# Two conditioned mixers with later parameter loads, new hand-written orders, and output splits on GpSimd

## What is computed

```
first_block, for each of 2 layers:
  x = layer_norm(ALPHA * x + 0.5 * swiglu_ffn(x, ffn1_w_gu[l], ffn1_w_down[l]), ...)
  x = layer_norm(ALPHA * x + hybrid_mixer(x, w_in[l], w_out[l], attn_sinks[l], ...), ...)
  x = layer_norm(ALPHA * x + 0.5 * swiglu_ffn(x, ffn2_w_gu[l], ffn2_w_down[l]), ...)
second_block, for each of 2 layers:
  mod = silu(c) @ w_ada[l] + b_ada[l];  shift, scale, gate = split(mod, 3)
  h = x * (1 + scale) + shift
  parts = split(h @ w_in[l], SPLIT_POINTS)
  o_a = mla_attention(...)        # latent attention, 6 heads
  o_b = dilated_attention(...)    # 6 heads
  o_c = sparse_attention(...)     # 4 heads, keys chosen by an indexer's top 64
  y = concatenate([o_a, o_b, o_c]) * silu(p_gate)
  x = layer_norm_2(ALPHA * x + (1 + gate) * (y @ w_out[l]), ln_g[l], ln_b[l])
```

## Time and profile before

| | us |
|---|---|
| median of 3 runs | 1343.25 (1341.85 to 1345.84) |
| the profiled execution, its own time | 1349.49 |
| its span, first to last instruction | 1347.7 |
| PE busy | 1321.4 (98%) |
| DVE busy | 1016.7 (75%) |
| ACT busy | 678.1 (50%) |
| POOL busy | 105.6 (8%) |
| DMA from HBM | 263.13 MB |

### The profile page before, as it was taken

One profiled execution on the slowest core, in us unless ns is written; L12 is line 12 of the kernel. 1 busy time (PEld: TensorE's weight loads), 2 busy tenths in 40 slices (PEclk: granted clock), 3 DMA queues, 4 the chain that ended last, 5 costly groups with the idle time before them and its releaser, 6 DMA issues.

```text
span 1347.7 us, 18984 instructions
## 1 busy us (share of the span) xinstructions
PE 1321.4 (98%) x7172; PEld 1119.2 (83%) x7172; DVE 1016.7 (75%) x1597; ACT 678.1 (50%) x1069; POOL 105.6 (8%) x153
## 2 busy tenths in 40 slices
PE   8999999999999999999999999999999999999997
PEld 7888888787888878888887888888888988798985
DVE  6676678886777777776778886687685689967887
ACT  6444445634544445344447445444355577456581
POOL 1011000011011100111010110111100000100000
PEclk9999999999999999999999999999998999999999
DMA  7976756437777557777564457777576443484530
GB/s 266 320 234 219 243 182 202 125 117 250 235 235 234 188 180 266 235 234 222 167 222 154 125 181 242 265 234 234 178 245 209 149 126 126 141 239 149 152 121 32
DMA packets 199402, 265.46 MB, mean 197 GB/s; under 512 B 21584, under 2 KB 144592, under 8 KB 198800
## 3 DMA queue, kind: packets, MB, share of 16 engines
q1 hardware_dynamic: 187600, 223.65, 51.8%
q0 software_dynamic: 11712, 40.60, 8.7%
HBM read 263.13 MB, written 1.07 MB: 196 GB/s over the span
## 4 chain that ended last, share of the span: by engine, by line
PE 84%; DVE 9%; DMA 4%; ACT 1%; issue 1%; SPq 0%; DVEq 0%; ACTq 0%
PE ps L791 26%; PE ps L793 25%; PE ps L792 25%; PE ps L860 4%; DVE w_lo L1266 3%; DMA w_raw<-in_w_in 2%; DMA w_raw<-in_ffn_w_gu 2%; PE ps L1004 1%; DVE arena L1557 1%; PE ps L1065 1%; PE ps L1039 1%; DVE small L1555 1%; DVE few_first L1295 1%; DVE y L1294 1%; ACT w_hi L1094 1%
## 5 line engine op out<-in xcount | busy, mean ns | idle before, releaser
L1266 DVE TENSOR_TENSOR w_lo<-w_raw,w_hi 128x1024 fp32r<-128x1024 f32 (+3 forms) x424 | 499.9, 1206 | 152.0 <-ACT w_hi L1094 148.9
L1094 ACT ACTIVATE w_hi<-w_raw 128x1024 fp32r<-128x1024 f32 (+3 forms) x424 | 432.5, 1046 | 244.5 <-DMA w_raw<-in_ffn_w_gu 126.2
L791 PE MATMUL ps<-w_hi,col_hi 128*128 128x512 f32 (+2 forms) x1024 | 396.3, 387 | 5.0 <-DVE w_lo L1273 2.6
L793 PE MATMUL ps<-w_hi,col_lo 128*128 128x512 f32 (+2 forms) x1024 | 391.3, 382 | 0.0
L792 PE MATMUL ps<-w_lo,col_hi 128*128 128x512 f32 (+2 forms) x1024 | 391.1, 382 | 0.0
L791 PEld LDWEIGHTS ps<-w_hi,col_hi 128*128 128x128 f32 x1024 | 192.7, 188 | 43.6 <-DVE w_lo L1266 4.6
L793 PEld LDWEIGHTS ps<-w_hi,col_lo 128*128 128x128 f32 x1024 | 192.4, 188 | 37.3
L792 PEld LDWEIGHTS ps<-w_lo,col_hi 128*128 128x128 f32 x1024 | 192.8, 188 | 34.0
L791 PE MATMUL ps<-w_hi,lat_hi 128*128 128x512 f32 (+2 forms) x544 | 209.0, 384 | 0.0
L793 PE MATMUL ps<-w_hi,lat_lo 128*128 128x512 f32 (+2 forms) x544 | 206.6, 380 | 0.0
L792 PE MATMUL ps<-w_lo,lat_hi 128*128 128x512 f32 (+2 forms) x544 | 206.3, 379 | 0.0
(11 more groups left out here) (148 smaller groups left out, 1182.9 us busy)
## 6 DMA issues: line engine op xcount, KB each, us to landing
w_raw<-in_ffn_w_gu SPq DMA_DIRECT2D x352, 256.0 KB, 4.4
w_raw<-in_w_in SPq DMA_DIRECT2D x108, 512.0 KB, 4.6
w_raw<-in_ffn_w_down SPq DMA_DIRECT2D x88, 512.0 KB, 4.9
mod<-in_w_ada POOLq DMA_DIRECT2D x32, 768.0 KB, 7.4
w_raw<-in_w_out SPq DMA_DIRECT2D x24, 512.0 KB, 4.6
norm_g<-in_ln_g POOLq DMA_DIRECT2D x8, 512.0 KB, 4.4
norm_b<-in_ln_b POOLq DMA_DIRECT2D x8, 512.0 KB, 6.0
w_raw<-in_w_out SPq DMA_DIRECT2D x16, 256.0 KB, 4.4
```

What stands on the lines that cost most here:

```text
L791: pe.matmul(dst, a_hi, b_hi, start=start, stop=False)
L793: return pe.matmul(dst, a_lo, b_hi, start=False, stop=stop)
L1094: act.activation(half_of(w_hi[j], n, h), half_of(raw[j], n, h), ACT.Copy).then_inc(hi_ready, 1)
L1266: tt(half_of(w_lo[j], n, h), half_of(raw[j], n, h), half_of(w_hi[j], n, h).bitcast(F32), ALU.subtract)\
```

## The change

It has five parts.

1. **Orders.** `MIX1_ORDER` and `MIX2_ORDER` are replaced. Mix1 keeps all its jobs. On PE its only exchanges are `trret:Q:0` with `score:W:2`, `trret:Q:1` with the three VR rows, and `row:GR:0:0` with `turn:W:2`. In mix2, PE's list changes in four places: `T:QI:0` goes ahead of `turn:B:0` and the VBX rows ahead of `score:B:0`; `mix:B:2` goes up, `trA:2` to `trA:5` come in a row, and `T:QC:1` comes between `score:A:1` and `turn:A:0` with `score:A:0` ahead of `T:QC:0`; `T:G:2` goes from ahead of `mix:A:2` and `turn:C:0` to behind them; at the end, both `xt` jobs of the next stage go ahead of `out:2:1` and `out:3:1`. The splits of ACT and DVE move with them, and high and low parts need no longer stand in the order of the units.
2. **GpSimd.** In mix2 the low parts of the four output units, eight halves, are subtracted by POOL (jobs `po:out/q:h`) with a semaphore of their own, and PE waits on that one for them. They stand in POOL's list ahead of and behind `modload`.
3. **params.** In mix2 the loads of gain and bias wait for `ropeA:0` instead of the translated x. In POOL's list `gateload` and `modload` stand behind them.
4. **table2.** It is loaded with the params of stage 5, an ffn stage, instead of at the start of stage 6. Stage 6's shift and scale therefore get a place in the arena instead of the table.
5. **Narrow pieces.** A piece of at most 64 columns is loaded whole with half 0. VBX has four transfers a unit instead of six, KI two instead of four, with the same bytes.

```diff
-hi:VBX/0:0 hi:VBX/0:1 row:L0:1:1 lo:QB/1:1 lo:QB/2:0 row:L1:1:0 row:L1:1:1 lo:QB/2:1 T:QB:0 xlate:0 hi:VBX/1:0
-lo:VBX/0:0 lo:VBX/0:1 sq:1 T:QB:1 lo:VBX/1:0 xlate:1 params hi:VBX/1:1 hi:QI/0:0 hi:QI/0:1 T:QB:2 latent:1
-trlat:0:0 trlat:0:1 hi:QI/1:0 hi:QI/1:1 score:B:0 lo:VBX/1:1 lo:QI/0:0 hi:KI/0:0 weigh:B:0 lo:QI/0:1 hi:KI/0:1
-row:VBX:0:0 trlat:1:0 trlat:1:1 row:VBX:0:1 row:VBX:1:0 row:VBX:1:1 lo:QI/1:0 lo:QI/1:1 turn:B:0 score:B:1 idxw:0
...
+hi:VBX/1:1 T:QB:0 T:QB:1 xlate:0 hi:QI/0:0 lo:VBX/1:0 latent:0 hi:QI/0:1 lo:VBX/1:1 lo:QI/0:0 xlate:1 lo:QI/0:1
+sq:1 T:QB:2 latent:1 params hi:QI/1:0 trlat:0:0 row:VBX:0:0 row:VBX:0:1 trlat:0:1 trlat:1:0 hi:QI/1:1 hi:KI/0:0
+row:VBX:1:0 score:B:0 lo:QI/1:0 trlat:1:1 hi:KI/0:1 row:VBX:1:1 hi:UQ/0:0 T:QI:0 hi:UQ/0:1 weigh:B:0 turn:B:0
...
+topk:0:0 topk:0:1 gateload topk:0:2 lo:QC/1:1 hi:G/0:0 trA:5 hi:G/0:1 hi:G/1:0 hi:G/1:1 topk:0:3 row:VC:1:0
+score:A:0 topk:1:0 T:QC:0 lo:G/0:0 topk:1:1 hi:G/2:0 weigh:A:0 score:A:1 lo:G/0:1 hi:G/2:1 topk:1:2 hi:G/3:0
+hi:G/3:1 T:QC:1 hi:out/0:0 turn:A:0 weigh:A:1 score:A:2 lo:G/1:0 lo:G/1:1 lo:G/2:0 hi:out/0:1 lo:G/2:1 T:G:0
+mix:A:0 lo:G/3:0 hi:out/1:0 turn:A:1 score:C:0 lo:G/3:1 weigh:A:2 weigh:C:0 T:G:1 mix:A:1 turn:A:2 topk:1:3
+score:C:1 po:out/0:0 mix:A:2 gate:1:0 weigh:C:1 gate:0:0 po:out/0:1 po:out/1:0 hi:out/1:1 turn:C:0 ycols:0:0
+T:G:2 T:G:3 gate:0:1 mix:C:0 gate:1:1 turn:C:1 +modload +fold gate:0:2 hi:out/2:0 ycols:1:0 ycols:1:1 mix:C:1
+ycols:0:1 ycols:0:2 po:out/1:1 po:out/2:0 po:out/2:1 po:out/3:0 hi:out/2:1 hi:out/3:0 out:0:0 gate:1:2 hi:out/3:1
+po:out/3:1 +lo:L0/0:0 out:1:0 out:2:0 +hi:L0/0:0 +hi:L0/0:1 out:3:0 ycols:1:2 norm:0 out:0:1 out:1:1 +hi:L0/1:0
...
                 for h in range(2):
-                    for q, (tensor, l, r0, c0, w, at_) in enumerate(pieces):
+                    for q in pieces_of((s, name), h):
+                        tensor, l, r0, c0, w, at_ = pieces[q]
...
+                        if w <= NARROW:
+                            tiles = slice(0, ks)
...
-                if kind == "params":
-                    if s > 0:
+                if kind == "po":
+                    n, h = NUMBER[job[1:3]], job[3]
+                    pool.wait_ge(hi_ready, at["high_part", job[1:]])
+                    pool.tensor_tensor(half_of(w_lo[SLOT[n]], n, h), half_of(raw[SLOT[n]], n, h),
+                                       half_of(w_hi[SLOT[n]], n, h).bitcast(F32), ALU.subtract).then_inc(po_ready, 1)
+                elif kind == "params":
+                    if KIND[s] == "mix2":
+                        pool.wait_ge(rope_a_done, at["ropeA", ("ropeA", s, 0)])
+                    elif s > 0:
                         pool.wait_ge(x_ready, at["x_ready", (s, 1, 1)])
...
+                    if s == FIRST2 - 1:
+                        pool.dma_start(table[:, 0:T2], t["table2"]).then_inc(tables_in, 16)
```

More of the change, by code:

```diff
@@ L208 @@
 MIX1_ORDER = """
[L209 to L218, removed]
@@ new lines @@
+score:W:1 hi:VR/0:1 weigh:W:0 row:KR:0:0 row:KR:0:1 row:KR:1:0 lo:VR/0:0 hi:VR/1:0 weigh:W:1 hi:VR/1:1 turn:W:0
+lo:VR/0:1 row:KR:1:1 lo:VR/1:0 hi:GR/0:0 hi:GR/0:1 mix:W:0 turn:W:1 lo:VR/1:1 rot:Q:0 hi:GR/1:0 hi:GR/1:1 params
+rot:Q:1 hi:out/0:0 row:VR:0:0 trret:Q:0 rot:K:0 lo:GR/0:0 attn:0 score:W:2 weigh:W:2 lo:GR/0:1 row:VR:0:1
+row:VR:1:0 row:VR:1:1 rot:K:1 trret:Q:1 trret:K:0 mix:W:1 hi:out/0:1 ret:0 row:GR:0:0 lo:GR/1:0 hi:out/1:0
+turn:W:2 lo:GR/1:1 lo:out/0:0 ret:1 mix:W:2 attn:1 retmix:0 gn:0 lo:out/0:1 trret:K:1 row:GR:0:1 ret:2 gnx:0
@@ L231 @@
[L231 to L245, removed]
+hi:L1/1:0 lo:L1/1:0 lo:L1/1:1 row:L0:0:0 row:L0:0:1 row:L1:0:0 hi:L1/1:1 xt:1:0 lo:QB/0:0 hi:QB/0:0 xt:1:1
@@ new lines @@
+lo:QI/1:1 lo:KI/0:0 lo:KI/0:1 score:B:1 lo:UQ/0:0 T:QI:1 weigh:B:1 hi:UQ/1:0 T:KI:0 hi:UQ/1:1 lo:UQ/0:1
+hi:UKV/0:0 score:B:2 weigh:B:2 mix:B:0 idxw:0 idxw:1 idx:0 turn:B:1 hi:UKV/0:1 hi:VC/0:0 lo:UQ/1:0 lo:UQ/1:1
+hi:VC/0:1 lo:UKV/0:0 row:UQ0:0:0 row:UQ0:1:0 hi:QC/0:0 mix:B:1 lo:UKV/0:1 hi:QC/0:1 idx:1 turn:B:2 lo:VC/0:0
+row:UQ1:0:0 row:UQ1:1:0 hi:QC/1:0 hi:QC/1:1 row:UV:0:0 lo:VC/0:1 lo:QC/0:0 row:UV:1:0 ropeA:0 ropeA:1 idx:2
+row:UK:0:0 ropeK:0 mix:B:2 ropeK:1 lo:QC/0:1 row:UK:1:0 trA:0 trA:1 row:VC:0:0 lo:QC/1:0 trA:2 trA:3 trA:4
@@ L339, in with_splits @@
         assert at <= first[u]
-        places[at] += [(kind, *u, h) for h in range(2) for kind in ("hi", "lo") if (kind, *u, h) not in placed]
+        places[at] += [(kind, *u, h) for h in range(2) for kind in ("hi", "lo")
+                       if (kind, *u, h) not in placed and (kind, ("po", *u, h)) not in {("lo", q) for q in placed}]
     return [q for p, job in zip(places, jobs) for q in p + [job]]
@@ L346, with pieces_of @@
 NUMBER = {u: n for n, u in enumerate(UNITS)}
-for kind_ in ("hi", "lo"):
-    assert [q[1:] for q in JOBS if q[0] == kind_] == [(*u, h) for u in UNITS[FIRST_UNITS:] for h in range(2)], "split in order"
+HALVES = [(*u, h) for u in UNITS[FIRST_UNITS:] for h in range(2)]
+for kinds_ in (("hi",), ("lo", "po")):
+    assert sorted(HALVES.index(q[1:]) for q in JOBS if q[0] in kinds_) == list(range(len(HALVES))), "each half is split once"
 SLOT = [n % SLOTS for n in range(len(UNITS))]
 AFTER = [n - SLOTS if n >= SLOTS else None for n in range(len(UNITS))]
+NARROW = 64
+def pieces_of(u, h):
+    return [q for q, piece in enumerate(unit_shape(*u)[2]) if h == 0 or piece[4] > NARROW]
 LANDINGS = []
@@ L353 @@
     before = [LANDINGS[m] for m in range(n_) if SLOT[m] == SLOT[n_]]
-    LANDINGS.append((before[-1] if before else 0) + (16 * len(unit_shape(*u_)[2]) if n_ >= FIRST_UNITS else 0))
+    LANDINGS.append([(before[-1][h_] if before else 0) + (16 * len(pieces_of(u_, h_)) if n_ >= FIRST_UNITS else 0)
+                     for h_ in range(2)])
 def gu_bank(s, r, i):
@@ L403, in count_jobs @@
             held, step, readers, stage, buffers = {}, None, {}, s, []
+        if kind in ("hi", "lo", "po"):
+            COUNT.add("low_part" if kind == "lo" else "pool_part" if kind == "po" else "high_part", job[1:])
         got = unit_of(job)
```

38 lines of the change are left out of this document (23 added, 15 removed).

## The result

The changed kernel took 1365.68 us in the median of 4 runs (1365.13 to 1366.23), the kernel before beside it 1344.55 us (4 runs, 1341.85 to 1349.59). The ratio is 1.0159, with a 95% interval of 1.0134 to 1.0183. The forecast was 1337.4 us with a range up to 1344.5: wrong in direction, and by 28.3 us. The profiled execution took 1365.8 us, its span is 1364.0 us, so it stands for the median, unlike the one of before, which lay 6.2 us above its own.

What follows compares the result with a forecast made beforehand. PE was taken as the bound, busy 1321.4 of 1347.7 us, leaving at most 26.3 us to win. Terms of -7.2, -2.8, -1.1, +2.8, +0.8 and +1.6 sum to -5.9 us: 1343.25 to 1337.4 us, range 1331.5 to 1344.5.

Steps and rivals of the forecast that it cites:

- R2: Rival, mix2 stages: POOL's subtractions and DVE's two-operand SBUF reads hold each other up; 1341.8 us, chance 0.18.
- B: At `turn:A:0`, both mix2 stages: two low parts fewer on DVE ahead of `weigh:A:0` remove a wait; -2.8 us.
- C: End of stage 6: eight low parts leave DVE, so the wait behind the next stage's norm goes; -1.1 us.
- A: At `turn:B:0`, both mix2 stages: later parameter loads and new order remove PE's wait and the lower clock; -7.2 us.
- D: New waits at `mix:A:2` and `turn:C:0` in both mix2 stages, as `T:G:2` no longer covers them; +2.8 us.
- E: Four `trA` in a row, mix2 stages: the third and fourth wait for ACT's copy of the bank; +0.8 us.
- F: Output products, mix2 stages: POOL's subtractions, taken at 2.4 us each, come 0.8 us late per stage; +1.6 us.
- R3: Rival: POOL's subtraction takes 4 us or more, PE waits at out/2:1 to out/3:1; 1350.2 us, chance 0.07.
- Mix1 and the loads: Mix1 stages and the parameter, table and narrow loads at their new places: no new PE waits, costed at 0.
- R4: Rival at `turn:B:0`: narrow pieces, not POOL's loads, delay QI/1, and KI lands late; 1341.4 us, chance 0.08.

Runs made afterwards that it cites:

- the memsets: Kernel without POOL's subtractions, plus 24 POOL fills in stage 7 that write SBUF, read nothing and serve nobody: 1339.53 us, one run.

## Why the prediction was wrong

**The step that failed is the price of R2.** The sum credits B and C with DVE's full relief and puts nothing for DVE being held up by POOL; that stands only in the rival R2, at 4.5 us. The mechanism was named there, with the two-operand instructions of DVE, and the mark by which to know it ("longer than their 1.22 us"). The SBUF — State Buffer page of the Trainium skill (Who interferes with whom) states an exclusive lock between a DVE instruction with two SBUF inputs and a GpSimd instruction that reads SBUF, not one that only writes it, and none for a DVE instruction with at most one, outside its 2-port modes. The traces agree on each point: 12.33 instead of 5.76 us, 5.76 under the memsets, 0.68 for the PSUM operand. What it costs is measured here alone: 25.3 us, where the text put 4.5 (1.1 + 1.4 + 2.0). Three things were mis-sized.

- *The lock doesn't cancel the relief, it outweighs it.* I let DVE lose as much as it was relieved of, 1.22 us for each low part. A page without any lock would show 1017.9 - 16 x 1.22 = 998.4 us for DVE; it shows 1034.8, so each subtraction by POOL holds DVE up for 36.4 / 16 = 2.3 us, nearly the whole of POOL's own duration. DVE is 1.1 us worse off for each low part given away.
- *Where it falls.* I spread the loss over the stage. Its largest piece, 6.57 us, falls ahead of `score:C:0`, on a chain DVE, ACT, DVE, PE without cover, and the three subtractions ahead of it were put there by the change.
- *The second price.* TensorE stood idle 6.4 us and then ran at 0.89 over 30 us, as it did in the earlier trace rows after 3.1 us. I had counted that price where it went (A), not where it might come: by the estimate above up to 4.8 of the 12.4 us.

The chance of 0.18 was too low as well. Where no row spoke for or against, the rule of the Trainium skill should have weighed more, and with its right price R2 would have set the upper end of the range.

**A (-7.2).** Right in cause, wrong in size. The wait behind line 1277 is gone in both stages, with the clock at 1.00. But I took it from an execution of 1349.49 us and carried the difference over whole to a median of 1343.25. The execution of 1340.02 us has neither the wait nor the lower clock, and alone the loads gave 1.2 us in the median: most of the 6.2 us between the two was, it seems, A itself. No execution at the median was profiled, so how much of A it holds stays open.

**B (-2.8).** The wait behind the division went, and 1.2 us of ACT's copies came at `mix:A:0` instead, as ACT's own order puts two splits ahead of them. Nothing is left.

**C (-1.1).** With POOL, the wait behind the norm is gone; without, it is 0.6 instead of 0.9 us, so the orders give 0.3.

**D (+2.8) and E (+0.8).** Without POOL, PE waits 0.4 us at `mix:A:2` and not at all at `turn:C:0`, so D is under a third of its size; the fourth `trA` in a row waits no longer than before, 0.3 us, so E is 0.

**F (+1.6).** The spacing is 3.3 us where the two engines alternate; single ones take 2.60 and 2.41 us where POOL is least disturbed, against 2.4 in the sum. R3's bound of 3.1 us was passed where they alternate, but PE comes to the outputs so late that POOL is late for it only once, in stage 7, for 3.0 us at most, and there together with DVE's split. The GPSIMD Engine Reference of the Trainium skill (Performance versus the Vector engine) led to an estimate of 2.25 us; the traces show 2.4 us at the least (stage 7, at 1327.99) and 2.99 us in the mean. At 2.25 us the sum of F itself would be 0.9 us less, not 0.6.

**Mix1 and the loads (0).** Right: 121.77 of 122.00 us in mix1, and no wait of PE for a transfer in either mix2 stage. Of R4 the price falls: nothing of the wait is left. Its other half, that the narrow pieces and not POOL's loads delay QI/1, was not tested, as every kernel with the loads moved has whole narrow pieces too; that the same pieces go ahead of it in the execution where it is in time speaks against it.

Without F the terms made -7.5 us, and the kernel without POOL's subtractions gave -3.4.

## What to carry to other kernels

Moving elementwise work from DVE to POOL relieves DVE only where POOL's reads don't meet DVE instructions with two operands in SBUF: compare POOL's duration with what DVE is spared (2.3 us lost here for 1.22 us spared), and look at what stands behind DVE at that place. What POOL only writes (24 memsets, 0.3 us), and DVE instructions with one operand in PSUM (0.68 us as ever), went side by side at no price here. And before a wait is priced from one profiled execution, see how that execution stands to the median: a gap as large as the term is a warning that the term is the gap.
